# Token stage, laps and combination in one block, the last pair of experts added by products: a transformer program on one core

## The chip, the core and the metric

The program runs on one core of a Trainium2 chip. The core has five engines with their own instruction streams, which meet only in semaphores: TensorE (matrix products; PE in the profile, PEld its weight loads), VectorE (DVE), ScalarE (ACT), GpSimd (POOL) and SyncE (SP), which issues most DMA transfers. A transfer runs on 16 DMA engines and raises a semaphore by 16 when it has landed. The metric is the time of the whole program on the device in microseconds, lower is better.

## The reference

A transformer: first a block with experts that choose their tokens, then two layers (i = 0, 1), each of a mixer and a layer of experts chosen by the tokens, on 512 tokens of width 1024. All is in float32. What this case is about is the end of each of the two layers:

```python
# 4 groups of 8 experts: the best group of a token, and in it its 2 best experts
gates = group_probability * softmax(two best logits)
y     = sum over the 2 choices: gate * (silu(x @ w_gate[e]) * (x @ w_up[e])) @ w_down[e]
x     = layer_norm(ALPHA * x + y) * ln2_g + ln2_b      # ALPHA = 4 ** 0.25
```

There are 32 experts of inner width 512. Each gets as many tokens as chose it; none may be dropped.

## The kernel before

The tokens are four tiles of 128 (`NT`), the rows of the stream X are kept in SBUF. The layer's end is three stages, each a block of five engine programs that ends with a clearing of its semaphores and a barrier of all engines (`stage`, to line 219).

**`token_stage`** (from line 1841) goes over 16 pairs of experts. An expert has 64 slots (`SLOTS`), three pairs have an uneven split. For each pair TensorE gathers the tokens into slots by products with one-hot matrices (line 2089), multiplies by the gate and up weights (line 2119), VectorE forms silu(gate)*up (line 2013), TensorE turns it (2155) and multiplies by the down weights (2135), and ScalarE copies the result to `ye` (2057). GpSimd then writes the 128 rows of the pair to the table `expert_rows` in memory with an indirect transfer (1968), whose rows VectorE has counted (`rows_of_slots`, 1979 to 1981). The table was filled with zeros once, earlier in the program. The weights, 2 MB for each third of an expert's pair, go through a ring of 6 places and two further places (`more`), eight in turn; of the last pair the up and down weights come in halves, the second halves last (line 1952). At the stage's start VectorE finds the places of the experts and, in `rows_of_choices`, the table's row of every choice of every token (`at_row`) and the number of laps. After the weights SyncE issues the next mixer's first two loads (`load_until`, line 181), then the gate weights that a first lap would use (line 1959), and waits until the last rows are stored.

**`extra_slots`** (from 2498) holds the laps: where an expert was chosen by more tokens than it has slots, each lap computes 64 further rows. Its code is there for all counts; the engines load the count (line 2538) and branch over it when it is zero (2539). With the inputs of this case it is zero in both layers.

**`combine_and_norm`** (from 2659): ScalarE computes the exponentials of the gates, GpSimd gathers for each tile and each of the two choices 128 rows of 4 KB from `expert_rows` (line 2693) into three buffers, so that the fourth tile waits for the first to be added. For each tile ScalarE scales the first choice's rows (2716), VectorE adds the second's (2758) and ALPHA * X with the sum for the mean (2760), ScalarE takes the squares and the root (2722, 2724), and VectorE centres (2769) and scales (2775). In the first layer TensorE then turns the rows into columns (2709), after three idle products for each tile (line 190), and ScalarE copies them to `xT` (2730), on which the next mixer's first matmuls (4032) depend. In the second layer SyncE stores the tiles as the result (2684).

## Time and profile before

| | |
|---|---|
| median of 3 runs | 2883.49 us (2882.11 to 2886.49) |
| profiled execution, its own time | 2882.69 us |
| its span, first to last instruction | 2880.9 us |
| TensorE busy | 2576.0 us, 89% |
| VectorE busy | 904.4 us, 31% |
| ScalarE busy | 615.1 us, 21% |
| GpSimd busy | 271.9 us, 9% |
| mean granted TensorE clock | 0.953 of full |

How to read it: the span is one execution, its stages one after the other, so that a share of busy time is a mean over stages with different limits. The end of the first layer lies at 1945 to 1993 us, that of the second at 2834 to 2881. In the 40 slices of the page TensorE is at 8 tenths or less around the first and at 3 tenths in the very last slice.

### The profile page before, as it was taken

The page shows a single profiled execution, that of the slowest core. Times are in us where ns is not written, and L with a number is a line of the kernel's source. Part 1 is how long each engine was busy: PE and PEld are TensorE (multiplying, and loading weights), DVE is VectorE, ACT ScalarE, POOL GpSimd, SP SyncE. Part 2 cuts the span into 40 slices and gives each one's busy share as a digit, 9 for nine tenths or more (in the row PEclk, how much of TensorE's full clock was granted, in tenths as well). Part 3 has the DMA queues.
Part 4 walks back from the last instruction along what each step waited for, and adds up shares of the span by engine and source line. Part 5 has one row for each costly group of instructions (what it writes and reads, how often), then busy time and mean ns, then how long its engine had stood idle before and what let it go on. Part 6 is the DMA issues. An engine that isn't in the chain of part 4 may idle for free. (4 is left out here: it accounts for less than half of the span.)

```text
span 2880.9 us, 42912 instructions
## 1 busy us (share of the span) xinstructions
PE 2576.0 (89%) x17839; PEld 1316.3 (46%) x17839; DVE 904.4 (31%) x1996; ACT 615.1 (21%) x1192; POOL 271.9 (9%) x251
## 2 busy tenths in 40 slices
PE   7998788989999989998899989895998889999893
PEld 3544687444334434445454434442356554444341
DVE  2655574231122112456450101003335461010003
ACT  4412444221000101233110101102323221111012
POOL 0100453200000000001110000001004110000001
PEclk9999798889999999999999999998999999999996
DMA  8222200859999993000559999995004129999995
GB/s 317 94 96 108 76 3 17 346 228 427 427 428 429 429 400 128 23 1 30 194 214 427 426 427 428 427 401 195 8 1 182 49 88 404 427 427 428 427 426 221
DMA packets 111216, 737.17 MB, mean 256 GB/s; under 512 B 24388, under 2 KB 27824, under 8 KB 71744
## 3 DMA queue, kind: packets, MB, share of 16 engines
q1 hardware_dynamic: 102688, 704.21, 59.6%
q0 software_dynamic: 7776, 29.37, 2.6%
q8 instruction: 135, 2.21, 0.3%
q10 hardware_dynamic: 576, 1.05, 0.1%
q14 instruction: 41, 0.34, 0.0%
HBM read 709.40 MB, written 33.57 MB: 258 GB/s over the span
## 5 line engine op out<-in xcount | busy, mean ns | idle before, releaser
L2119 PE MATMUL bank<-ring,expert_in 128*64 128x512 f32 (+1 forms) x1792 | 343.2, 600 | 21.9 <-DMA ring<-in_moe_w_up_dram 21.2
L2013 DVE TENSOR_TENSOR hidden<-silu_gate,bank 128x512 f32<-128x512 f32 x32 | 33.7, 1053 | 630.2 <-PE bank L2119 396.8
L2119 PEld LDWEIGHTS bank<-ring,expert_in 128*64 128x64 f32 (+1 forms) x1792 | 113.3, 131 | 245.8 <-issue 245.5
L2135 PE MATMUL bank<-ring,hidden_T 128*64 128x512 f32 (+1 forms) x896 | 170.0, 595 | 31.0 <-ACT hidden_T L2053 31.0
L2089 PE MATMUL bank<-onehot,x_part 128*128 128x128 bf16 x3072 | 178.0, 220 | 0.0
L1747 PE MATMUL bank<-ring,expert_in 128*64 128x512 f32 x768 | 169.8, 598 | 4.9 <-DMA ring<-in_w_gate_dram 4.9
L2089 PEld LDWEIGHTS bank<-onehot,x_part 128*128 128x128 bf16 x3072 | 173.2, 98 | 1.6 <-issue 1.0
L2037 ACT ACTIVATE expert_in<-bank 128x512 f32<-128x512 f32 x64 | 35.0, 595 | 416.9 <-PE bank L2089 416.9
L2881 PE MATMUL bank<-ring,home 128*128 128x512 f32 x256 | 119.2, 628 | 3.5 <-PEq L219 3.5
L1968 POOL DMA_INDIRECT expert_rows<-expert_out,row_of_slot x32 | 31.3, 977 | 920.1 <-ACT expert_out L2057 920.1
L2119 PE MATMUL bank<-home,expert_in 128*64 128x512 f32 (+1 forms) x256 | 114.4, 600 | 0.0
L3225 PE MATMUL bank<-x_cols,ring 128*128 128x512 f32 x256 | 112.5, 593 | 1.3 <-PEq L219 1.3
L2135 PEld LDWEIGHTS bank<-ring,hidden_T 128*64 128x64 f32 (+1 forms) x896 | 52.1, 129 | 133.4 <-issue 96.7
L637 PE MATMUL bank<-home,ring 128*128 128x512 f32 (+1 forms) x320 | 111.7, 508 | 0.6 <-PEq L219 0.6
L1747 PEld LDWEIGHTS bank<-ring,expert_in 128*64 128x64 f32 x768 | 55.5, 138 | 116.5 <-issue 105.2
L4032 PE MATMUL bank<-x_cols,ring 128*128 128x512 f32 (+2 forms) x224 | 99.2, 608 | 1.4 <-PEq L219 1.4
L1762 PE MATMUL bank<-ring,hidden_T 128*64 128x512 f32 x384 | 85.9, 604 | 1.2 <-ACT hidden_T L1652 1.2
L2057 ACT ACTIVATE expert_out<-bank 128x512 f32<-128x512 f32 x64 | 34.7, 595 | 233.2 <-PE bank L2135 233.2
L682 PE MATMUL bank<-ring,home 128*128 128x512 f32 x192 | 84.4, 596 | 0.0
L190 PE MATMUL bank<-const 128*128 128x512 f32 x98 | 57.8, 733 | 28.7 <-DVE home L2760 24.7
L637 PEld LDWEIGHTS bank<-home,ring 128*128 128x128 f32 x320 | 60.5, 190 | 49.7 <-issue 45.9
L2881 PEld LDWEIGHTS bank<-ring,home 128*128 128x128 f32 x256 | 51.3, 203 | 68.4 <-issue 68.4
(684 smaller groups left out, 3907.4 us busy)
## 6 DMA issues: line engine op xcount, KB each, us to landing
ring<-in_moe_w_gate_dram SPq DMA_DIRECT2D x50, 2048.0 KB, 22.0
ring<-in_moe_w_down_dram SPq DMA_DIRECT2D x48, 2048.0 KB, 27.4
ring<-in_moe_w_up_dram SPq DMA_DIRECT2D x44, 2048.0 KB, 26.0
ring<-in_w_gate_dram SPq DMA_DIRECT2D x24, 2048.0 KB, 22.0
ring<-in_w_up_dram SPq DMA_DIRECT2D x24, 2048.0 KB, 21.1
ring<-in_w_down_dram SPq DMA_DIRECT2D x24, 2048.0 KB, 26.6
ring<-in_w_mod_dram SPq DMA_DIRECT2D x12, 2048.0 KB, 10.2
home<-in_moe_w_gate_dram SPq DMA_DIRECT2D x8, 2048.0 KB, 24.1
```

The costliest lines, as they stand in the source:

```text
L190: pe.matmul(self.psum[bank][:, :], self.c("ident"), self.const[:, 0:4, :], start=True, stop=True)
L637: mm = pe.matmul(B[g % 4][:, 0:SEGS[r][1]], m.slot(n)[:, k, f % 4 * P:f % 4 * P + P], aT[:, k, where[r]], start=(k == 0), stop=(k == NC - 1))
L682: mm = pe.matmul(B[g % 4][:, :], aT[:, k, t * P:(t + 1) * P], m.slot(m.in1[4 + s])[:, k, :], start=(k == 0), stop=(k == NC - 1))
L1747: mm = pe.matmul(B[2 + 2 * part + b][rows, :], xe[:, dc, rows], ws[e][:, c, b * COLS:(b + 1) * COLS], start=(dc == 0), stop=(dc == NC - 1))
L1762: mm = pe.matmul(B[6 + b][rows, :], hT[:, fc, rows], ws[e][:, c, b * COLS:(b + 1) * COLS], start=(fc == 0), stop=(fc == NF - 1))
L2037: return act.activation(xe[:, 4 * c:4 * c + 4, :], B[c][:, :].rearrange("p (c s) -> p c s", c=4), ACT.Copy)
L2089: mm = pe.matmul(B[c // 4][:, c % 4 * P:(c % 4 + 1) * P], src[part][:, t, c * P:(c + 1) * P], oh[:, t, :, :], start=(k == 0), stop=(k == 3 ...
L2119: mm = pe.matmul(B[2 + 2 * part][rows, :], xe[:, c, rows], ws[e][:, c, :], start=(c == 0), stop=(c == NC - 1))
L2135: mm = pe.matmul(B[6 + b][rows, :], hT[:, c, rows], ws[e][:, c, b * COLS:(b + 1) * COLS], start=(c == 0), stop=(c == NF - 1))
L2881: mm = pe.matmul(B[2 * (t % 2) + a][:, :], lhs(k)[:, t * P:(t + 1) * P], m.slot(n)[:, k, :], start=(k == 0), stop=(k == NC - 1))
L3225: mm = pe.matmul(B[g % 2][:, :], m.slot(n)[:, k, h * P:(h + 1) * P], xT[:, k, :], start=(k == 0), stop=(k == NC - 1))
L4032: mm = pe.matmul(B[job % 2][rows[0]:rows[1], :], m.slot(n)[:, k, at:at + size], xT[:, k, :], start=(k == 0), stop=(k == NC - 1))
```

## The change

The three stages become one, with one barrier at its end. In it:

- The gates and `rel`, the place of each choice relative to the last pair's slots, are computed at the start of the stage.
- The last pair isn't written to memory. VectorE builds for each tile a matrix of 128 tokens by 128 slots that holds the gate where a choice is in that slot (`last_onehots`), TensorE turns it (into `last_T`), and `scatter_last` multiplies it with `ye`. Its rows in the table stay zero.
- X is multiplied by ALPHA in the last pair. `choices` adds gate times the gathered row to it, directly for each choice; `add` then adds the products of the last pair from two banks, with the sums for the mean.
- The gathers go to the two places of the ring that the last pair doesn't use. The two of the first tile wait for the rows of the second to last pair to be stored; those of the other three also wait for the last pair's last weights to land.
- The laps' branch stands between the last pair and the combination in the program of every engine but GpSimd; a lap now adds its rows by products too. The first lap's weights are no longer loaded ahead.
- SyncE loads gain and shift of the norm after the last weights, and the next mixer's first two loads only when all gathered rows are added (`presummed`).
- One idle product fewer for each tile ahead of the transposes. Centring, scaling and square roots are as before; a square root without use loads its table ahead.

The diff, cut to its core (the code of a lap, the two removed functions, names and semaphores are left out):

```diff
-def token_stage(m, w, E, first_load, R, out_rows, first_lap, more, i):
+def token_stage(m, I, w, E, first_load, R, out_rows, more, i, X, xT=None, out=None):
...
+        at_row, g01, rel = R.at_row, R.g01, Q[0]
+        dead = K[1][:, :, :].rearrange("p a b -> p (a b)")
+        last_oh = dead[:, 0:NT * P].rearrange("p (t s) -> p t s", t=NT)
+        lane_last, last_tmp = dead[:, NT * P:(NT + 1) * P], dead[:, (NT + 1) * P:(NT + 2) * P]
+        last_T = act_g
...
+        place_of = lambda j: m.ring[:, (first_load + j) % RING, :]
+        y = [place_of(j).rearrange("p (t d) -> p t d", t=NT) for j in range(2)]
+        sq = more[1][:, 4:6, :].rearrange("p a b -> p (a b)")
+        spare = [a[:, :, :].rearrange("p c t -> p (c t)") for a in more]
+        held = [[place_of(j) for j in (2, 3, 4)], [place_of(5)] + spare]
...
+        def laps_beyond(eng, lap):
+
+            eng.wait_ge(laps_known, 2)
+            total = eng.value_load(R.count[0:1, 0:1], min_val=0, max_val=MOST_LAPS)
+            with eng.If(total > 0):
+                lap(total, 0, 0)
+                with eng.Fori(0, MOST_LAPS // 2 - 1) as k:
+                    with eng.If(total > 2 * k + 1):
+                        lap(total, 2 * k + 1, 1)
+                    with eng.If(total > 2 * k + 2):
+                        lap(total, 2 * k + 2, 0)
+                eng.nop()
...
+                laps_beyond(sp, lap)
+                sp.dma_start(gain, I["ln2_g_2"][i].partition_broadcast(P)).then_inc(ln_here, 16)
+                sp.dma_start(shift, I["ln2_b_2"][i].partition_broadcast(P)).then_inc(ln_here, 16)
+                sp.wait_ge(presummed, NT)
                 m.load_until(sp, end + 2)
-                sp.wait_ge(laps_known, 2)
-                e = sp.value_load(R.count[0:1, 1:2], min_val=0, max_val=E - 1)
-                sp.wait_ge(m.weights_used, base + loads * pairs - loads + 1)
-                src_w, chunks, cols = expert_loads(wg, wu, wd, e)[0]
-                sp.dma_start(first_lap[:, 0:chunks * cols].rearrange("p (c f) -> p c f", c=chunks), src_w).then_inc(m.lap_gate, 16)
-                sp.wait_ge(stored, 16 * pairs + stored_here)
+                sp.wait_ge(stored, 16 * (pairs - 1) + stored_here)
+                sp.wait_ge(ln_here, 32)
+                if out is not None:
+                    for t in range(NT):
+                        sp.wait_ge(shifted, t + 1)
+                        sp.dma_start(out[t * P:(t + 1) * P, :], X[:, t, :]).then_inc(out_stored, 16)
+                    sp.wait_ge(out_stored, 16 * NT)
...
-                for x in range(pairs):
+                for x in range(pairs - 1):
...
+                pool.wait_ge(gates_ready, 2)
+                pool.wait_ge(stored, 16 * (pairs - 1) + stored_here)
+                for t in range(NT):
+                    if t == 1:
+                        for e in range(2):
+                            _, last_here, before = home(loads * pairs - 2 + e, 1, 1)
+                            pool.wait_ge(last_here, 16 * (before + (loads * pairs - 1) // WIDE + 1))
+                    for j in range(2):
+                        pool.indirect_dma_start(y[j][:, t, :], None, out_rows[:, :],
+                                                bass.IndirectOffsetOnAxis(ap=at_row[:, t, j:j + 1], axis=0)).then_inc(here[2 * t + j], 16)
...
+                def last_onehots():
+
+                    dve.wait_ge(gathered, pairs)
+                    lo = Order(dve, last_order)
+                    dve.tensor_copy(lane_last[:, 0:SLOTS], R.lane[:, 0:SLOTS])
+                    lo.then(dve.tensor_scalar(lane_last[:, SLOTS:], R.lane[:, 0:SLOTS], float(SLOTS), None, ALU.add))
+                    for t in range(NT):
+                        dve.tensor_scalar(last_oh[:, t, :], lane_last, rel[:, t, 0:1], g01[:, t, 0:1], ALU.is_equal, ALU.mult)
+                        lo.then(dve.tensor_scalar(last_tmp, lane_last, rel[:, t, 1:2], g01[:, t, 1:2], ALU.is_equal, ALU.mult))
+                        last = dve.tensor_tensor(last_oh[:, t, :], last_oh[:, t, :], last_tmp, ALU.add)
+                        if t < NT - 1:
+                            lo.then(last)
+                        else:
+                            last.then_inc(last_ready, 1)
+                    for t in range(NT):
+                        dve.tensor_scalar(X[:, t, :], X[:, t, :], ALPHA, None, ALU.mult).then_inc(stretched, 1)
+
                 def pair(x):
-                    rows_of_slots(x)
-                    if not isinstance(x, int) or x < pairs - 1:
+                    if isinstance(x, int) and x == pairs - 1:
+                        last_onehots()
...
+                order.then(dve.tensor_tensor(rel[:, :, :], Q[0][:, :, :], Q[1][:, :, :], ALU.add))
+                order.then(dve.tensor_scalar(rel[:, :, :], rel[:, :, :], 1.0 - (E - 2) * SLOTS, None, ALU.add))
+                go = Order(dve, gate_order)
+                dve.wait_ge(exped, 2)
+                go.then(dve.tensor_reduce(mass[:, :, 0], R.below[:, :, :], AX_X, ALU.add))
+                go.then(dve.scalar_tensor_tensor(den[:, :, :], R.second[:, :, :], 1.0, mass[:, :, :], ALU.add, ALU.mult))
+                dve.reciprocal(g01[:, :, 0:1], den[:, :, :]).then_inc(gates_ready, 1)
+                dve.wait_ge(gates_ready, 1)
+                dve.tensor_tensor(g01[:, :, 1:2], g01[:, :, 0:1], R.second[:, :, :], ALU.mult).then_inc(gates_ready, 1)
+                dve.wait_ge(gates_ready, 2)
...
+                laps_beyond(dve, lap)
+                no = Order(dve, norm_order)
+
+                def choices(t):
+                    for j, told in enumerate((accumulated, presummed)):
+                        dve.wait_ge(here[2 * t + j], landed)
+                        if j == 0:
+                            dve.wait_ge(stretched, t + 1)
+                        else:
+                            dve.wait_ge(accumulated, t + 1)
+                        dve.scalar_tensor_tensor(X[:, t, :], y[j][:, t, :], g01[:, t, j:j + 1], X[:, t, :], ALU.mult, ALU.add).then_inc(told, 1)
+
+                def add(t):
+                    dve.wait_ge(presummed, t + 1)
+                    dve.wait_ge(scattered, t + 1)
+                    for h in range(2):
+                        cut = slice(h * COLS, (h + 1) * COLS)
+                        dve.scalar_tensor_tensor(X[:, t, cut], X[:, t, cut], 1.0, B[2 * (t % 2) + h][:, :], ALU.mult, ALU.add,
+                                                 accum_out=total[:, t, h:h + 1]).then_inc(summed, 1)
+                    dve.wait_ge(summed, 2 * t + 2)
+                    no.then(dve.tensor_tensor(minus[:, t:t + 1], total[:, t, 0:1], total[:, t, 1:2], ALU.add))
+                    dve.tensor_scalar(minus[:, t:t + 1], minus[:, t:t + 1], -1.0 / D, None, ALU.mult).then_inc(mean_ready, 1)
...
+                choices(0)
+                choices(1)
+                add(0)
+                choices(2)
+                add(1)
+                centre(0)
+                finish(0)
+                choices(3)
+                add(2)
+                centre(1)
+                finish(1)
+                add(3)
+                centre(2)
+                finish(2)
+                centre(3)
+                finish(3)
...
+                        act.wait_ge(last_turned, 1)
+                        act.activation(last_T[:, :], B[1][:, :], ACT.Copy).then_inc(last_T_ready, 1)
...
+                act.activation(R.below[:, :, :], R.below[:, :, :], ACT.Exp).then_inc(exped, 1)
+                act.activation(R.second[:, :, :], R.second[:, :, :], ACT.Exp).then_inc(exped, 1)
...
+                laps_beyond(act, lap)
...
+                act.activation(mass[:, 0, :], m.eps[:, 0:1], ACT.Sqrt)
+                root(0)
...
+                        pe.wait_ge(last_ready, 1)
+                        for t in range(NT):
+                            mm = pe.transpose(B[1][:, t * P:(t + 1) * P], last_oh[:, t, :], m.c("ident"))
+                        mm.then_inc(last_turned, 1)
...
+                laps_beyond(pe, lap)
+
+                def scatter_last(t):
+                    if t >= 2:
+                        pe.wait_ge(summed, 2 * (t - 1))
+                    for h in range(2):
+                        mm = pe.matmul(B[2 * (t % 2) + h][:, :], last_T[:, t * P:(t + 1) * P], ye[:, h * COLS:(h + 1) * COLS], start=True, stop=True)
+                    mm.then_inc(scattered, 1)
+
+                def turn_rows(t):
+                    if t >= 2:
+                        pe.wait_ge(x_copied, 2 * (t - 1))
+                    m.idle_products(pe, 4 + 2 * (t % 2), 2)
+                    pe.wait_ge(shifted, t + 1)
+                    for h in range(2):
+                        for c in range(4):
+                            at = (4 * h + c) * P
+                            mm = pe.transpose(B[4 + 2 * (t % 2) + h][:, c * P:(c + 1) * P], X[:, t, at:at + P], m.c("ident"))
+                        mm.then_inc(x_turned, 1)
+
+                pe.wait_ge(last_T_ready, 1)
+                pe.wait_ge(out_ready, pairs)
+                for t in range(NT):
+                    scatter_last(t)
+                    if xT is not None and t >= 2:
+                        turn_rows(t - 2)
+                if xT is not None:
+                    turn_rows(2)
+                    turn_rows(3)
...
-        whole = (m.moe2[i] + (E // 2) * len(pair_loads(*w, 0)) // WIDE * RING + 2) % RING
-        free = [m.ring[:, (whole + k) % RING, :] for k in range(4)]
-        held = [free[0:3], [free[3], own[:, :, :].rearrange("p c t -> p (c t)"), cols[:, :, :].rearrange("p c t -> p (c t)")]]
-        token_stage(m, w, E, m.moe2[i], R, S["rows"], held[0][0], more, i)
-        extra_slots(m, w, E, R.parts, R.lane, R.at_row, R.count, S["rows"], held, 16 * (i + 1))
-        combine_and_norm(m, I, i, S["rows"], R, X, cols, **ends)
+        token_stage(m, I, w, E, m.moe2[i], R, S["rows"], more, i, X, **ends)
```

## Rows read from the trace of the kernel before

**Rows 1.** the chain that ended last: start us, us, engine and line

```profile
2846.69 8.22 DMA chosen_rows<-expert_rows,row_of_choice
...
2856.27 1.29 DVE chosen_rows L2758
...
2857.59 1.24 DVE home L2760 x2
...
2874.76 1.28 DVE home L2769
...
2876.15 1.28 DVE home L2775
```

**Rows 2.** instructions by time, second layer's end: start us, us, engine, line

```profile
2834.35 0.59 PE L2135 MATMUL bank<-home,hidden_T 128*64 128x512 f32 x1
2835.01 1.08 ACT L2057 ACTIVATE expert_out<-bank 128x512 f32<-128x512 f32 x2 [7.21 <-PE bank L2135]
...
2877.46 0.33 SPq L2684 DMA_DIRECT2D out_dram<-home  x1
```

**Rows 3.** the same, first layer's end and the next mixer

```profile
1945.42 1.09 ACT L2057 ACTIVATE expert_out<-bank 128x512 f32<-128x512 f32 x2 [7.21 <-PE bank L2135]
...
1987.32 1.28 DVE L2775 SCALAR_TENSOR_TENSOR home<-home,ln_var 128x1024 f32<-128x1024 f32 x1
...
1990.73 1.08 ACT L2730 ACTIVATE x_cols<-bank 128x512 f32<-128x512 f32 x2 [2.88 <-PE bank L2709]
...
1992.54 19.98 PE L4032 MATMUL bank<-x_cols,ring 128*128 128x512 f32 x46 [1.42 <-PEq L219]
```

**Rows 4.** lines 2538 and 2539: ns min/median/max, first and last start us

```profile
L2538 PEldq TENSOR_LOAD <-laps x2: 315/401/487, 1952.5 to 2841.1; - x2
...
L2539 DVEq COMPARE_BRANCH  x2: 62/62/63, 1953.1 to 2841.7; - x2
...
L2539 PEldq COMPARE_BRANCH  x2: 3349/3430/3512, 1953.3 to 2841.8; - x2
```

**Rows 5.** instructions by time, start of the first layer's token stage

```profile
1491.09 0.90 DVE L2003 TENSOR_TENSOR onehot<-slot_lane,pair_slots 128x128 bf16<-128x128 f32 x4
...
1494.67 0.25 PE L2081 MATMUL bank<-one_bf,onehot 128*128 128x1 bf16 x4
```

**Rows 6.** lines 2990 and 392: VectorE from a bank, and scaling

```profile
L2990 DVE SCALAR_TENSOR_TENSOR home<-home,bank x16: 686/688/690, 1395.6 to 2344.2; 128x512 f32<-128x512 f32 x16
...
L392 DVE TENSOR_SCALAR x_rows<-x_rows,opening_rs x6: 749/750/753, 13.4 to 16.9; 128x1024 f32<-128x1024 f32 x6
```

**Rows 7.** DMA issues at 2813, 1958 and 2861 us: last number us to landing

```profile
expert_rows<-expert_out,row_of_slot POOLq DMA_INDIRECT x1, 7.9
...
chosen_rows<-expert_rows,row_of_choice POOLq DMA_INDIRECT x1, 7.8
...
chosen_rows<-expert_rows,row_of_choice POOLq DMA_INDIRECT x2, 5.3
```

**Rows 8.** issue of the last weights and their us to landing, both layers

```profile
2798.79 1.73 SPq L1952 DMA_DIRECT2D home<-in_moe_w_down_dram  x1
...
home<-in_moe_w_down_dram SPq DMA_DIRECT2D x1, 1024.0 KB, 29.5
...
1910.38 4.10 SPq L1952 DMA_DIRECT2D home<-in_moe_w_down_dram  x1
...
home<-in_moe_w_down_dram SPq DMA_DIRECT2D x1, 1024.0 KB, 30.0
```

**Rows 9.** stretches: busy of each engine, granted clock, DMA share, GB/s

```profile
2820.00:2825.00 5.00, 5.00 (x26) 1.45 (x22) 0.00 (x0) 0.00 (x0) 0.00 (x0) 1.00 1.02 424
...
2837.00:2840.00 3.00, 0.00 (x0) 0.00 (x0) 0.00 (x0) 0.00 (x0) 0.93 (x1) 0.52 0.15 56
...
1970.00:1973.00 3.00, 2.96 (x4) 1.42 (x5) 2.91 (x6) 2.76 (x5) 2.44 (x2) 0.50 0.37 127
```

**Rows 10.** DMA issue of the next mixer's first weights at 1921.9 us

```profile
ring<-in_od_w_in_dram SPq DMA_DIRECT2D x1, 1664.0 KB, 22.8
```

438 lines of the change are left out of this document (177 added, 261 removed).

## The prediction

> **What bounds the kernel now.** I began with the chain that ended last [rows 1]: the kernel ends in the combination of the second layer of token-choice experts, a series of VectorE instructions fed by a gather that lands 8.2 us after its issue at 2846.69. Next I read the instructions in order of time around that gather [rows 2]. The last product of the last expert pair starts at 2834.35, ScalarE copies it out at 2835.01, and the first addition of the combination begins only at 2856.27. So 21 us lie between the end of the products and the first useful addition, with TensorE idle. They hold the copy (1.1 us), the scatter of the last pair's rows to memory, two stage boundaries and the skipped lap code, and the 8.2 us of the gather. From 2856.27 VectorE is the bound until 2877.43, and the result's last store ends the span 3.47 us later. The first of the two layers has the same tail [rows 3]: copy at 1945.42, last VectorE instruction ends at 1988.60, next matmul of the following mixer at 1992.54. Nothing else in the program touches these two stretches, so the change is worth what it takes out of them, twice, plus or minus what it puts into the last pair and the start of the stage.
>
> One row explains most of the boundary: TensorE's branch over the lap code takes 3.43 us, behind a register load and checks of 0.6 us, where VectorE's takes 0.06 [rows 4]. No lap runs with this data (no matmul of a lap is in the trace), so all laps are only jumped over.
>
> **The change part by part.** All times are on the profiled run's scale; T0 is the moment when the first `add` of the new combination starts.
>
> Removed: the last scatter, two boundaries and their barriers, the load of the first lap's weights (2 MB a layer, read by nobody here), four ScalarE scalings.
>
> Start of the stage. VectorE gets two small instructions for `rel` and four for the gates, at about 0.2 us with their waits, 1.25 us. Before, it finished the second pair's one-hots at 1491.99 and TensorE asked for them at 1494.67 [rows 5]: 2.7 us of cover, 1.4 left. ScalarE's two exponentials and their table fall before the first half gathered. Cost 0; without that cover 1.25 us a layer.
>
> Last pair. `last_onehots` is 14 small instructions (about 3 us) and four scalings of X at 0.75 us [rows 6], 6 us, in a stretch where VectorE waited 22 us for the up products. TensorE's four transposes (0.66 us for four like them) sit in front of the hidden's transposes, for which it waited 1.3 us anyway; ScalarE's copy `last_T` falls beside the down products. Cost 0.
>
> The gathers of the first tile wait for the second to last pair's scatter, 7.9 us after its issue at 2813.6 [rows 7], so about 2821.5. They put 1 MB on engines that were full with weights: the last weights landed at 2798.79+29.5 = 2828.3 and at 1910.38+30.0 = 1940.4 [rows 8]. At the 424 GB/s of that stretch [rows 9] their 1.05 MB are 2.5 us. The delay of the last weights is thus between 0 and 2.5; I take 2.5, since the scatter beside full queues shows that the two share (7.9 us against 5.3 for a gather almost alone [rows 7]). The second halves of the down weights are wanted only in the middle of the products, near 2831.3, so TensorE doesn't stall at 2830.8. The page "DMA: Bandwidth & Descriptors" of the Trainium skill (SWDGE vs HWDGE vs iDMA) says that each DMA engine takes turns between the two kinds of queue; by that the gather gets its share at once and the weights pay the 2.5 us, while an order by issue would cost them nothing.
>
> The other six gathers queue on GpSimd behind the wait for these weights. Nothing else is on GpSimd, and VectorE waits for them. The second of tile 1 is issued 1.27 us after 2830.8, lands after 8.2 us [rows 1] (the layer-norm loads, 1 MB, now arrive at the same moment as before), and its addition takes 1.28: **2841.5**. In the first layer the same sum from 1940.4 is 1942.9+1.27+7.8 [rows 7]+1.28 = **1953.2**. Bounds: no delay and 5.3 us give 2836.2 and 1948.3.
>
> TensorE's path to the first addition: after the last product (2834.35) the 0.6 us and the branch of 3.43 [rows 4], then the two products of `scatter_last(0)`. A float32 product of 512 columns is two records, 0.43 us each at the upper clock (46 in 19.98 us [rows 3]), 0.87 at the lower. The granted clock had fallen to 1.2 GHz (0.52 of full) between 2837 and 2840 [rows 9], so I take the lower: 3.5 us. 2834.35+4.0+3.5 = **2841.9**; in the first layer 1944.76+4.0+3.5 = 1952.3. Bounds: no stall in the branch and the upper clock give 2836.1+1.9 = 2838.0; a fetch twice as long, since its transfer now meets gathers, gives 2845.3. The page "Runtime: NRT & Kernel Launch" (Instruction fetch mechanics) says that a taken branch to a target outside the loaded instructions waits for a fetch; by it the skip, now longer, stalls TensorE again, and perhaps VectorE and ScalarE too.
>
> So T0 is 2842.0 and 1953.2: two paths that arrive within 1 us of each other.
>
> Chain from T0, VectorE without a gap: four `add` at two 0.69 us instructions from a bank [rows 6] with accumulation and 0.35 for the mean, 1.75 each; two `choices` still to come (tiles 2 and 3), 2x1.32 us by the spacing of 2856.27 and 2857.59 [rows 1]; four centre and finish, 2.65 each (2874.76 to 2877.43 [rows 1]). 7.0+5.3+10.6 = 22.9. Before it was 21.2: the additions of two tiles have gone ahead of T0, but those of the other two and the bank additions stay in it.
>
> Second layer: 2842.0+22.9+3.47 = 2868.4 against 2880.9, **-12.5**. First layer: 1953.2+22.9 = 1976.1; the tail after VectorE was 3.94 us (1988.60 to 1992.54 [rows 3]), of which 1.2 go with one idle product fewer ahead of the last transposes: 1978.8 against 1992.54, **-13.7**. The next mixer's first weights (`load_until(end + 2)`) are now issued after the last `choices`, T0+11.4 = 1964.6, on idle engines; 14 us are left for 1.8 MB, so nothing.
>
> Sum: -26.2. The profiled run's own time was 2882.7, 0.8 below the median of the runs: 2856.5+0.8 = **2857**.
>
> **The rivals.**
> (a) Both paths to T0 arrive at their lower bounds: 2838.0 and 1948.3, so -16.5 and -18.6: **2848**. For it: the lap load is gone and the transfers total the same, and a branch costs 0.05 us on the others. Against: the 3.43 us were seen twice.
> (b) The branch's fetch takes twice as long beside gathers, and TensorE enters the next mixer at the lower clock for some 2.5 us: -9.2, -11.2, +2.5, **2866**.
> (c) The next mixer's weights decide. They took 22.8 us to land before [rows 10], behind full queues. From 1964.6 that is 1987.4: the first layer keeps only -5.1, **2866**. Against it: nothing else is on the queues then.
> (d) The change doesn't do what it says: the gathers don't run ahead of the end of the products but start when the rows are out, 2836. Then T0 is 2849.5 (8.2, 1.27 and two `choices` later) and about 1959.5: **2871**.
> (e) Slower than before: TensorE goes through the new tail in short pieces and the granted clock doesn't come back when the next mixer starts. Its matmuls then take twice their time; from 26 us of full-speed work done at half speed the gain is gone, and with 30 it is **2887**. Against: after 24 idle us, at the lower clock from 1970 to 1973 [rows 9], the clock was back before the next mixer.
>
> **How the numbers follow.** The forecast has 0.72; (a) 0.11, (b) 0.06, (c) 0.04, (d) 0.02, (e) 0.03, and 0.02 that it stays within 0.2%. A measurement of this kernel can tell 0.2% (5.8 us) from no change. The own range of the likeliest, one or two steps of the two paths early or late, is 2850 to 2863; with most of (a) and (b) it is 2848 to 2865. Faster 0.95, same 0.02, slower 0.03.
>
> **What would show it.** Right: one stage where three were; the first gather issued near 2821 and 1932, the third near 2831 and 1943; a TensorE branch of 3.4 us right behind the last down product; VectorE without gaps from the first bank addition on. The steps to check first are the landing of the last weights, the branch, the clock in `scatter_last(0)`, and whether the mixer's first matmul waits for its weights. The prediction is wrong if the last pair's own products wait for weights, or if VectorE stands still inside the 22.9 us.

## The result and the profile after

The changed kernel took 2847.4 us (median of four runs, 2844.2 to 2849.2), the kernel before 2883.7 on the same chip: ratio 0.9872, 95% interval 0.9855 to 0.9889. That is a gain of 36 us where 26 were predicted, and just outside the range (2848). On two more chips the same pair gave 0.9888 (0.9871 to 0.9906) and 0.9886 (0.9865 to 0.9906). The mean of the three ratios, 0.9882, is 34 us; so the first comparison showed a little too much, and the prediction (0.9908) was still 7 to 8 us short.

The page of the changed kernel, sections 1 and 3 (busy time; DMA queues with packets, MB and share):

```profile
span 2842.4 us, 42947 instructions
...
PE 2583.4 (91%) x17871; PEld 1320.7 (46%) x17871; DVE 929.7 (33%) x2064; ACT 607.8 (21%) x1188; POOL 269.8 (9%) x249
...
q1 hardware_dynamic: 102400, 700.01, 60.0%
q0 software_dynamic: 7488, 29.10, 2.6%
```

The profiled run took 2844.2 us itself, 3.2 under its median, against 2882.7 before: 38.5 us between the two profiles. The end of the chain that ended last, in the profile after (start, us, engine and line):

```profile
2774.13 32.77 DMA home<-in_moe_w_down_dram
2807.03 3.67 PE bank L2394 x16
2812.63 3.29 PE bank L2486 x4
2816.03 1.32 DVE home L2207 x4
2817.65 1.29 DVE home L2200
...
2836.91 1.28 DVE home L2224
```

and the same stretch by instructions, with the idle time ahead of them and who ended it:

```profile
2800.45 0.66 PE L2414 MATMUL bank<-const,rank_pairs 128*128 128x128 f32 x4
...
2807.03 0.61 PE L2394 MATMUL bank<-spare_weights,hidden_T 128*64 128x512 f32 x1 [0.29 <-DMA home<-in_moe_w_down_dram]
...
2810.73 1.08 ACT L2270 ACTIVATE expert_out<-bank 128x512 f32<-128x512 f32 x2 [7.21 <-PE bank L2394]
...
2812.63 7.08 PE L2486 MATMUL bank<-expert_out,silu_gate 128*128 128x512 f32 x12 [1.95 <-ACT expert_out L2270]
...
2813.20 2.67 DVE L2200 SCALAR_TENSOR_TENSOR home<-ring,gate,home 128x1024 f32<-128x1024 f32 x2 [2.89 <-DMA ring<-expert_rows,row_of_choice]
...
2816.03 0.69 DVE L2207 SCALAR_TENSOR_TENSOR home<-home,bank 128x512 f32<-128x512 f32 x1
...
2838.22 0.33 SPq L2037 DMA_DIRECT2D out_dram<-home  x1
```

To be seen: the last weights release TensorE's second half of the down products (2807.03, the line of [rows 8]). ScalarE's copy starts at 2810.73, TensorE's products that scatter the last pair at 2812.63, and the first bank addition (T0) at 2816.03, 5.3 us after the copy's start, where the kernel before needed 21 us to its first addition [rows 1, 2].

For everything that follows a layer's end is cut at four marks: the first of the last down products, ScalarE's copy of the last pair, T0, and VectorE's last instruction; behind it comes the next mixer's first product (first layer) or the end of the span (second layer). The expectations below call the part from the copy on a tail. Of the 38.5 us between the two profiles, 16.3 lie from the copy to the next mixer in the first layer (47.1 to 30.9) and 14.2 from the copy to the end in the second (45.9 to 31.7), 30.5 together. The other 8 lie where the prediction had put nothing: 2.7 ahead of the first of these copies and 5.4 in the mixer, router and token work between the two ends (842.5 to 837.1). Of those 5.4, 3.3 are one stretch of the mixer. Windows of before and after over the same work (busy of each engine, granted clock, DMA share, GB/s):

```profile
2032.00:2056.00 24.00, 24.00 (x56) 11.30 (x56) 17.64 (x21) 3.73 (x5) 0.00 (x0) 0.86 0.00 1
```

```profile
2013.00:2034.00 21.00, 21.00 (x57) 10.32 (x56) 16.41 (x19) 3.87 (x6) 0.00 (x0) 1.00 0.00 1
```

TensorE is busy all the time in both; the clock was 0.86 of full in one and full in the other. So three things are open: whether these 8 us belong to the change, why T0 comes 5.3 us behind the copy and not 7.0, and what the branch, the gathers' landing and the order of the transfers have to do with it.

### The profile page after: what moved, and what is told of

It is laid out like the page before. It is cut to its first block and busy times, and to the rows that moved or that the text cites. A ratio compares the mean times of both kernels' runs of the same rounds, so it can differ in the third digit from the quotient of the medians.

```text
span 2842.4 us, 42947 instructions
## 1 busy us (share of the span) xinstructions
PE 2583.4 (91%) x17871; PEld 1320.7 (46%) x17871; DVE 929.7 (33%) x2064; ACT 607.8 (21%) x1188; POOL 269.8 (9%) x249
## 5 line engine op out<-in xcount | busy, mean ns | idle before, releaser
L2394 PEld LDWEIGHTS bank<-ring,hidden_T 128*64 128x64 f32 (+1 forms) x896 | 52.1, 129 | 133.4 <-issue 96.7
L636 PEld LDWEIGHTS bank<-home,ring 128*128 128x128 f32 x320 | 60.5, 190 | 49.7 <-issue 45.9
L1572 DVE TENSOR_TENSOR home<-home,bank 128x512 f32<-128x512 f32 x64 | 43.8, 687 | 119.9 <-PE bank L1773 119.9
## 6 DMA issues: line engine op xcount, KB each, us to landing
ring<-in_moe_w_gate_dram SPq DMA_DIRECT2D x48, 2048.0 KB, 22.9
```

Source lines behind the costliest of these rows:

```text
L636: mm = pe.matmul(B[g % 4][:, 0:SEGS[r][1]], m.slot(n)[:, k, f % 4 * P:f % 4 * P + P], aT[:, k, where[r]], start=(k == 0), stop=(k == NC - 1))
L1572: dve.tensor_tensor(X[:, t, cut], X[:, t, cut], B[4 + dh][:, :], ALU.add).then_inc(added, 1)
L2394: mm = pe.matmul(B[6 + b][rows, :], hT[:, c, rows], ws[e][:, c, b * COLS:(b + 1) * COLS], start=(c == 0), stop=(c == NF - 1))
```

## The experiments

Each kernel is compared with the kernel before on its own chip. The times of a single kernel spread over 5 to 19 us here (the changed kernel on the third chip: 2843.2 to 2858.3), more than most effects asked for, so the verdicts rest on the marks of the profiles, one profile for each altered kernel. This table has them all, in us; the first column of each layer is the whole end, from the first last-down product on. The changed kernel's own three profiles differ by up to 1.3 us in one of these columns and by 1.5 in the last. The four kernels from "all gathers wait" to "last pair through the table" ran on a chip that has no profile of the changed kernel.

| kernel | ratio (95%) | layer 1: end | copy to T0 | layer 2: end | copy to T0 | both ends |
|---|---|---|---|---|---|---|
| before | | 54.3 | | 53.0 | | 107.3 |
| before, second profile | | 56.8 | | 55.5 | | 112.3 |
| changed | 0.9872 (0.9855-0.9889) | 38.7 | 6.0 | 39.3 | 5.3 | 78.0 |
| changed, second | 0.9888 (0.9871-0.9906) | 37.8 | 5.1 | 39.6 | 4.9 | 77.4 |
| changed, third | 0.9886 (0.9865-0.9906) | 37.4 | 4.7 | 39.1 | 5.0 | 76.6 |
| branch bare | 0.9923 (0.9907-0.9939) | 43.2 | 10.5 | 46.2 | 11.9 | 89.4 |
| layer-norm loads late | 0.9900 (0.9883-0.9917) | 40.4 | 7.8 | 39.4 | 6.0 | 79.8 |
| all gathers wait | 0.9903 (0.9879-0.9927) | 39.3 | 7.3 | 40.7 | 7.2 | 80.0 |
| no gather waits | 0.9894 (0.9872-0.9917) | 38.8 | 5.8 | 41.3 | 7.1 | 80.1 |
| lap load back | 0.9902 (0.9879-0.9925) | 40.6 | 7.9 | 43.5 | 9.8 | 84.1 |
| last pair through the table | 0.9916 (0.9894-0.9937) | 42.8 | | 44.5 | | 87.3 |
| free gathers, new order | 0.9879 (0.9856-0.9902) | 36.7 | 5.8 | 40.1 | 7.2 | 76.9 |
| the same, warm | 0.9871 (0.9850-0.9892) | 36.1 | 5.7 | 37.6 | 5.9 | 73.7 |
| the same, no branch | 0.9879 (0.9857-0.9900) | 37.8 | 3.7 | 39.0 | 3.7 | 76.9 |

(The second profile of before is of one run that took 2892.9 us, just above what that kernel took in eleven runs beside it, 2878.1 to 2891.9. Its ends are longer by 1.7 us a layer because the first of its last down products ran at a lower clock: 8.9 us from the first of them to the copy, not 7.2.)

**Is the rest of the gain the change's?** Both kernels once more, unaltered.

> The changed kernel once more, unaltered. Open: the 5.4 us that the profiles show in the mixer, router and token work between the two tails (842.5 before, 837.1 after) and 2.7 us ahead of the first tail. If they belong to the change (a clock that comes back sooner in the next mixer), this profile shows the same: from the first layer's copy of the last pair plus its tail to the second layer's last copy again 837 us. If they are chance of one execution, that stretch is anywhere between 836 and 843 and the dip of the clock seen before at 2032 to 2056 appears or not without rule. Time 2847 in either case, ratio 0.987.

> The kernel before once more, unaltered, for a second profile. If the dip of the granted clock (0.86 between 2032 and 2056, worth 3.3 us) belongs to the longer idle tail, it is there again and the stretch between the tails is again 842 us; if it is chance, this profile has it elsewhere or not, and the stretch is between 836 and 843.

The stretch between the two ends took 842.5 and 843.2 us in the two profiles of before, and 837.1, 842.1 and 842.1 in the three of the changed kernel; in the other kernels of the table, all with the new ends, anything from 836.3 to 841.7. The copy of the first layer started at 1945.4 and 1953.3 before, at 1942.8, 1948.5 and 1938.1 after. So the same kernel differs from itself by 5 us between the ends and by 8 to 10 ahead of them. The 2.7 us ahead of the ends are within that. The 3.3 us in the mixer are chance: to one and the same ScalarE instruction behind the dip (`gate_abs`) it was 65.5 and 63.8 us from the mixer's first product before, and 62.1, 65.5 and 65.5 in the changed kernel. But the stretch as a whole isn't shown to be chance: all twelve profiles with the new ends are shorter there (mean 839.4) than both profiles of before (mean 842.9). Some 3.5 us may belong to the change; two profiles of before are few, and what would cause it is open. Between copy and next mixer or end it is 93.0 and 94.6 us before against 62.5, 61.2 and 60.9 after: 31 to 34.

**Where does the branch lie?**

```diff
+                pe.wait_ge(out_ready, pairs)
                 laps_beyond(pe, lap)
```

> TensorE waits for ScalarE's copy of the last pair before it enters the skipped lap code; nothing else is changed. Theory A (the sequencer runs ahead of its products, so the branch of 4.7 to 5.2 us lay beside the last products and beside the copy): the branch now begins at the copy's end, 1.1 us after the last product, and the first product of the last pair's scatter comes 3.4 to 5 us later, the whole chain of VectorE with it: +7 to +10 us over both layers, 2854 to 2857. Theory B (the branch begins behind the last product, as my prediction had it, and cost its 4 us already): it moves by the copy's 1.1 us at most and so does the start of the additions: +0 to +2, 2847 to 2849.

TensorE's branch over the lap code in the second layer, in the changed kernel and then with the wait; ns, and when it started:

```profile
L1964 PEldq COMPARE_BRANCH  x1: 4664/4664/4664, 2807.8 to 2807.8; - x1
```

```profile
L1964 PEldq COMPARE_BRANCH  x1: 5982/5982/5982, 2820.9 to 2820.9; - x1
```

and the instructions behind it, in the kernel with the wait:

```profile
2827.03 2.90 PE L2487 MATMUL bank<-expert_out,silu_gate 128*128 128x512 f32 x3 [8.09 <-issue]
...
2830.89 0.69 DVE L2207 SCALAR_TENSOR_TENSOR home<-home,bank 128x512 f32<-128x512 f32 x1 [7.08 <-PE bank L2487]
```

In the changed kernel the branch starts 2.9 us before the copy does, while the last down products still run; it ends at 2812.5, 0.7 us after the copy's end. Put behind the copy, it delays the scatter's products by its whole length: T0 comes 10.5 and 11.9 us after the copy instead of about 5, both ends 12 us longer, the ratio 0.0035 (10 us) worse. Theory A, above its bounds (7 to 10); the branch itself took 4.5 and 6.0 us. TensorE's sequencer runs ahead of its products: the register load ahead of the branch started at 2807.1, right when the wait for the last weights was passed and 3.6 us before the copy could start.

**What sets the landing of the second tile's gathers?**

```diff
                 laps_beyond(sp, lap)
+                for e in range(2):
+                    _, last_here, before = home(loads * pairs - 2 + e, 1, 1)
+                    sp.wait_ge(last_here, 16 * (before + (loads * pairs - 1) // WIDE + 1))
                 sp.dma_start(gain, ...)
```

> The loads of the layer norm's gain and shift (1 MB a layer) are issued only when the last weights have landed, at the same moment as the gathers of the second tile. Theory A (these gathers landed in 5.5 us and not in the 8.2 predicted because the layer-norm loads, issued 28 us earlier, were through by then): the gathers of the second tile take about 8 us to land, and the last weights land up to 2.5 us earlier; the start of the additions moves by +0 to +2.7 a layer, total 2847 to 2853. Theory B (the landing has nothing to do with these loads; the second scatter and lap load that are gone made the difference): 5.5 us again, start of the additions where it was or 0 to 2 us earlier, total 2843 to 2847.

The two gathers of the second tile, first layer, in the changed kernel's second profile and then with late layer-norm loads (last number: median us to landing):

```profile
ring<-expert_rows,row_of_choice POOLq DMA_INDIRECT x2, 5.1
```

```profile
ring<-expert_rows,row_of_choice POOLq DMA_INDIRECT x2, 8.0
```

8.0 us beside these loads, 5.1 without: theory A. In the second layer it is 7.1 to 7.7 against 4.8 and 5.5. T0 came 7.8 and 6.0 us after the copy, where the prediction had 7.8 and 7.0 for the changed kernel. Not all of that is the gathers': the branch took 6.9 and 6.4 us in this kernel, and both paths to T0 were late by the same amount. Both ends together are 2.5 us longer than in the changed kernel (77.3, mean of three), all of it in the first layer; in the second the last weights landed 31.0 us after their issue, without a stall, and that paid for the later T0.

**Was the removed lap load worth nothing?**

```diff
+                sp.wait_ge(laps_known, 2)
+                e = sp.value_load(R.count[0:1, 1:2], min_val=0, max_val=E - 1)
+                sp.wait_ge(m.weights_used, base + loads * pairs - loads + 1)
+                sp.dma_start(lap_weights(0, 0), expert_loads(wg, wu, wd, e)[0][0]).then_inc(lap_extra, 16)
                 laps_beyond(sp, lap)
                 sp.dma_start(gain, ...)
```

> The load of the first lap's weights (2 MB a layer, read by nobody here), which the change had removed and which my prediction priced at nothing, is put back in its old place, ahead of the layer-norm loads. Theory A (its bytes push what is behind it): the layer-norm loads land 4 to 5 us later, together with the gathers of the second tile, which then take about 8 us to land as they did beside the late layer-norm loads; the start of the additions moves by 2 to 3 us a layer: total +4 to +6 against the changed kernel. Theory B (priced rightly at nothing): landing of these gathers 4.5 to 6.5 us as before, total unchanged within 2 us.

SyncE's DMA issues in the second layer of this kernel (start, us to issue):

```profile
2786.08 3.41 SPq L2012 DMA_DIRECT2D home<-in_moe_w_down_dram  x1
2805.79 0.33 SPq L2031 DMA_DIRECT2D ring<-in_moe_w_gate_dram  x1
2806.95 0.34 SPq L2033 DMA_DIRECT2D ln_gain_and_shift<-in_ln_g_dram  x1
```

and of the changed kernel:

```profile
2774.13 4.02 SPq L2011 DMA_DIRECT2D home<-in_moe_w_down_dram  x1
2778.97 3.15 SPq L2028 DMA_DIRECT2D ln_gain_and_shift<-in_ln_g_dram  x1
```

and what the gather of the second tile then takes in the chain of the kernel with the load:

```profile
2821.04 10.47 DMA ring<-expert_rows,row_of_choice
2832.73 1.31 DVE home L2213 x4
```

10.5 us to landing, T0 7.9 and 9.8 us after the copy, both ends 6.8 us longer than the mean of the three profiles of the changed kernel (77.3). Theory A, above what it expected (4 to 6). The rows show a part that neither theory had: the lap load waits on SyncE for the first products of the last pair to free its place, 16 us after the weights ahead of it, and the layer-norm loads stand behind it. Taking it away took 2 MB from the engines, and it also let 1 MB of other loads start 16 us earlier (4.8 us after the last weights' issue instead of 20.9). How the 6.8 us divide is not shown. Layer-norm loads that were later still (the run above) cost 2.5 alone, and the 2 MB themselves were under way beside the gathers: in the first layer the lap load was issued at 1931.4 and landed 19.0 us later, at 1950.4, when the second tile's gathers (1945.3 and 1946.6) were out.

```profile
ring<-in_moe_w_gate_dram SPq DMA_DIRECT2D x1, 2048.0 KB, 19.0
```

So the larger part is probably the bytes, the smaller the queue. The timed runs, 0.9902 against 0.9872 to 0.9888, are right in sign and don't resolve it.

**Do the gathers have to wait for the weights?**

```diff
-                    if t == 1:
+                    if t == 0:
                         for e in range(2):
                             _, last_here, before = home(loads * pairs - 2 + e, 1, 1)
                             pool.wait_ge(last_here, ...)
```

> The gathers of the first tile wait for the last weights too; nothing else changes. Measured by the tails: from ScalarE's copy of the last pair to the next mixer's first product (30.0 and 30.9 us in two profiles of the changed kernel) and from the copy to the end (31.7 and 31.2). Theory A (the first tile's megabyte pushes the last weights back by 2 to 3 us): the weights now land after about 29.5 us instead of 32 to 33, TensorE's stall in the last down products is gone, and since the gathers start that much earlier after the products the start of the additions moves by less than 1.5 us: tails within 1.5 us of before, total within 3 us of the changed kernel. Theory B (the weights are late for another reason): they land after 32 to 33 us again, and the second tile's gathers, now third and fourth in the line, come 2.5 us later: tails +2.5 each, total +5.

The last weights landed 31.3 us after their issue in the second layer (32.8 to 33.2 in the changed kernel), the stall in the down products (0.3 to 1.0 us) was gone, T0 moved from 5 to 7.2 us after the copy, and both ends are 2.7 us longer together. From the copy on, as the theories were put, it is 2.0 and 2.1 us a layer: between A (under 1.5) and B (2.5), with the weights between them too; they gained 1.5 to 1.9 us of the 3 that A gave them. Nor need the late landing be all the gathers' doing: in the second profile of before the last weights of that layer took 31.4 us with no gather beside them.

With the wait left out altogether:

```diff
-                    if t == 1:
-                        for e in range(2):
-                            _, last_here, before = home(loads * pairs - 2 + e, 1, 1)
-                            pool.wait_ge(last_here, ...)
```

> No gather waits for the last weights: all eight are issued as soon as the second to last pair's rows are stored. Theory A (weights and gathers share the engines by bytes): 3 MB more meet the last weights, which land 3 to 7 us later, and TensorE stalls that long in the middle of the last down products. VectorE's order keeps two of its additions behind the start, so nothing is won there but the 1 us that the second tile's gathers had cost: total +4 to +12 against the changed kernel. Theory B (the weights' queue goes ahead of the gathers): weights as before, 32 to 33 us, no stall beyond 0.5 us, start of the additions 4 us after the copy instead of 5 to 6: total -2 to -4.

TensorE went on with the last weights 32 and 33 us after their issue, as in the changed kernel, and not 3 to 7 us later: theory A failed. The DMA queues between 2807.7 and 2814.5, in which six gathers were issued while the last weights were under way (packets, MB, share of the engines' time):

```profile
q1 hardware_dynamic: 294, 1.41, 50.6%
q0 software_dynamic: 361, 1.34, 49.9%
...
ring<-expert_rows,row_of_choice POOLq DMA_INDIRECT x6, 12.5
```

The two kinds of queue had half of the engines' time each. The page "DMA: Bandwidth & Descriptors" of the Trainium skill (SWDGE vs HWDGE vs iDMA) says that an engine takes turns between them; this trace agrees. Why six more gathers hardly delay the weights is seen in the same 7 us of both kernels, from 8 to 1 us before the weights land: in the changed kernel with the first tile's two gathers,

```profile
q1 hardware_dynamic: 325, 1.69, 58.6%
q0 software_dynamic: 241, 0.90, 34.1%
```

and with all gathers free:

```profile
q1 hardware_dynamic: 315, 1.60, 55.5%
q0 software_dynamic: 317, 1.19, 43.9%
```

Two gathers took a third of the engines' time and left some of it unused. Eight took that too, and little of the weights' share: 1.60 MB against 1.69. They land 12 us after their issue instead. But theory B's gain (-2 to -4) didn't come either: the ends are 2.8 us longer. What is late is the branch:

```profile
L1964 PEldq COMPARE_BRANCH  x1: 5998/5998/5998, 2815.8 to 2815.8; - x1
```

6.0 us here and 5.2 in the first layer, against 3.4 to 5.2 (six branches, mean 4.1) in the changed kernel; it ends 1.4 and 2.0 us after the copy. During each branch the profile has one or two packets, 16 KB each, on the queue that it calls instruction; that they wait among the gathers is inferred from the branch's length, not seen. The page "Runtime: NRT & Kernel Launch" of the Trainium skill (Instruction fetch mechanics) says that a taken branch out of the loaded window waits for its fetch. TensorE's branches agree, with 3.4 us where the DMA engines were nearly idle and up to 6.9 beside full queues. The load isn't the only cause: in the second profile of before one took 4.8 us with the engines busy 5% of the time.

```profile
L2539 PEldq COMPARE_BRANCH  x2: 3564/4166/4767, 1960.3 to 2851.3; - x2
```

**How much is the block, how much the products?**

```diff
-                for x in range(pairs - 1):
+                for x in range(pairs):
                     pool.wait_ge(rows_known, x + 1)
...
-                pool.wait_ge(stored, 16 * (pairs - 1) + stored_here)
+                pool.wait_ge(stored, 16 * pairs + stored_here)
...
-                    scatter_last(t)
...
-                        dve.scalar_tensor_tensor(X[:, t, cut], X[:, t, cut], 1.0, B[2 * (t % 2) + h][:, :], ALU.mult, ALU.add,
-                                                 accum_out=total[:, t, h:h + 1]).then_inc(summed, 1)
```

The one-hots of the last pair, their transposes and their copy go too, and VectorE takes a tile's choices, mean, centre and finish in turn.

> One block as in the change, but the last pair again goes through the table: its rows are scattered, and all eight gathers wait for that; no products scatter it, and VectorE has no additions from a bank. It tells how much of the gain is the block and how much the products. By the rows of the changed kernel: copy's end to the scatter's landing 1 + 5.3 us, two gathers issued and landed 7, so the first addition comes 14.5 us after the copy's start + 1.1; then VectorE has 8 additions (10.6), four means and four centre and finish (11.4): copy to the last VectorE instruction 37.6 against 27.3 to 28.1, so each tail +9 to +10, total +19, ratio 0.995 to 0.996. If the block alone had brought most of the gain, the tails would be longer by under 5 us each; if it had brought nothing, by 15.

Both ends 87.3 us, 10 longer than in the changed kernel and 20 shorter than before: the block brought two thirds of what the ends gave (20.0 of 30.0 us against the first profile of before), and the products, with the early gathers that they allow, one third. I had expected 19 and a ratio of 0.995 to 0.996, and it is 0.9916. GpSimd in the second layer of this kernel:

```profile
2826.31 0.98 POOL L2046 DMA_INDIRECT expert_rows<-expert_out,row_of_slot  x1 [22.31 <-ACT expert_out L2252]
2829.72 0.97 POOL L2056 DMA_INDIRECT ring<-expert_rows,row_of_choice  x1 [2.42 <-DMA expert_rows<-expert_out,row_of_slot]
```

and VectorE's first addition there:

```profile
2834.05 1.28 DVE L2189 SCALAR_TENSOR_TENSOR home<-ring,gate,home 128x1024 f32<-128x1024 f32 x1 [18.21 <-DMA ring<-expert_rows,row_of_choice]
```

A scatter with nothing beside it landed in 2.6 us, not the 5.3 that I had taken from a gather, and the first gather in 4.3; the first addition comes 9.7 us after the copy, not 15.6.

**A faster version?** Three kernels on one chip with the changed kernel. The first lets all gathers go and adds the third tile's choices ahead of the first bank addition:

```diff
-                    if t == 1:
-                        for e in range(2):
...
                 choices(1)
+                choices(2)
                 add(0)
-                choices(2)
```

> No gather waits for the last weights, and VectorE adds the third tile's choices ahead of the first bank addition instead of behind it; nothing else changes against the changed kernel. The run with free gathers alone had its sixth gather on GpSimd issued at 1943.1 and 2811.5 and landing 11 to 12 us later, and the first bank addition at 1956.4 and 2825.8, held by TensorE's branch and products. Theory A (the third tile's rows are there by then and the chain behind gets two additions, 2.7 us, shorter, 22.2 to 19.5): tails of 28.0 and 30.8 us (copy to the next mixer's first product, copy to the end) against 30.0 to 30.9 and 31.2 to 31.7 in the changed kernel: total -3 to -4. Theory B (gathers issued earlier only land later, so the third tile's choices now hold the first bank addition up): tails as in the changed kernel or 1 us longer, total within 2 us.

28.9 and 32.1 us from copy to next mixer and to the end: the first layer 0.7 to 2 us shorter, the second 0.5 to 0.9 longer. Between the theories. The chain from T0 was 20.4 and 20.7 us where 19.5 was worked out. The windows behind the last down products of the second layer (busy of each engine, granted clock, DMA share, GB/s) show why:

```profile
2814.00:2816.00 2.00, 0.66 (x4) 0.00 (x0) 1.05 (x2) 1.27 (x3) 0.00 (x0) 1.00 0.94 373
2816.00:2818.00 2.00, 0.00 (x0) 0.00 (x0) 1.90 (x2) 1.30 (x2) 0.00 (x0) 0.75 0.72 287
2818.00:2820.00 2.00, 1.97 (x3) 0.96 (x4) 1.90 (x3) 0.00 (x0) 0.00 (x0) 0.50 0.33 135
```

TensorE stood still behind the last down products, and its clock was at the lower of its levels (0.50) when the scatter's products began; VectorE waited for them inside the chain. The second kernel gives TensorE work there:

```diff
+                m.idle_products(pe, 4, 2)
                 laps_beyond(pe, lap)
```

> As the run before in this series (free gathers, third tile first), and TensorE makes two idle products right behind the last down products, ahead of the skipped lap code, so that it works while ScalarE copies and its sequencer waits for the branch. Theory A (the granted clock falls to its lower level in the 2 us of idleness behind the last down products, and that doubles the first products of the last pair's scatter): from the first product of the scatter to the first bank addition it is 1.9 us instead of 3.2 to 3.9, the tails are 1.3 to 1.9 us shorter each, total -3 against the free-order kernel. Theory B (the clock falls all the same, or the rows of the third tile arrive last): no change in the start of the additions, total within 1 us.

```profile
2811.00:2813.00 2.00, 2.00 (x7) 0.68 (x4) 1.23 (x2) 1.16 (x3) 0.00 (x0) 1.00 0.96 385
2813.00:2815.00 2.00, 0.70 (x2) 0.00 (x0) 1.88 (x2) 1.42 (x2) 0.00 (x0) 1.00 0.73 291
2815.00:2817.00 2.00, 1.80 (x5) 0.88 (x6) 1.90 (x3) 0.00 (x0) 0.00 (x0) 1.00 0.31 127
```

The clock stayed at full, the chain was 19.5 us in both layers, and the ends are 3.2 us shorter together than in the kernel without the idle products, 2.9 to 4.3 shorter than in the changed kernel. TensorE's gap ahead of the scatter, without and then with the idle products (second layer):

```profile
2818.03 4.61 PE L2482 MATMUL bank<-expert_out,silu_gate 128*128 128x512 f32 x5 [3.37 <-issue]
```

```profile
2815.20 3.24 PE L2483 MATMUL bank<-expert_out,silu_gate 128*128 128x512 f32 x7 [1.50 <-issue]
```
From the scatter's first product to T0 it was 3.0 and 2.5 us, not 1.9: now the third tile's rows hold T0. By the timed runs the ratio is 0.9871 (0.9850 to 0.9892) beside 0.9886 (0.9865 to 0.9906) for the changed kernel on that chip; the intervals overlap, so the 3 us are seen in the marks of one profile and not in the time.

The third leaves TensorE's lap code out of that kernel; with this data no lap runs, so nothing of the computation is missing.

> As the warm kernel, and TensorE's lap code is left out, its branch with it (a kernel for this data only: no lap runs, the result doesn't need it). It tells what the branch still costs. In the run with free gathers it took 5.2 and 6.0 us and ended 1.4 and 2.1 us after ScalarE's copy. Theory A (what sticks out of the cover is all that it costs): the first product of the scatter comes within 0.2 us of the copy's end, the tails are 0 to 2 us shorter than in the warm kernel, less where the third tile's rows arrive last: total -1 to -4. Theory B (the branch costs its whole 4 to 5 us): tails shorter by 4 each, total -8.

T0 comes 3.7 us after the copy in both layers instead of 5.7 and 5.9, which looks like theory A, with 2 us for what stuck out. But the end as a whole was 77, not 70 us: in this profile TensorE stalled 2.8 us for the last weights in both layers (34.4 and 35.7 us to landing) and then ran its products at a clock of 0.74:

```profile
2825.00:2830.00 5.00, 5.00 (x17) 1.59 (x18) 2.36 (x3) 0.04 (x1) 0.00 (x0) 0.74 0.72 291
```

The median, 2850.1, shows no gain over the warm kernel's 2847.2. Nor do the 2 us belong to the branch for certain. In the warm kernel the third tile's rows held T0, and taking the branch out doesn't by itself make them earlier; here the late weights moved the copy to 11.3 and 11.6 us behind the issue of these rows' last gather, where it had been 7.3 and 7.6, so that they were there in time. What the branch still costs is thus open. Why the weights came later I can't say; it was one profile, of the slowest of this kernel's six runs. It does show the gathers ahead there: in the last 7.8 us before the weights landed they had 76.1% of the engines' time in the second layer and the weights' queue 25.3%, against 47.9% and 52.1% in the warm kernel.

The profile of the changed kernel on this chip, whose copy to T0 and ends are in the table:

> The changed kernel unaltered, on the same chip as the three above, for their comparison: tails of 30 to 31 and 31 to 32 us, the stretch between the tails anywhere from 836 to 843, ratio between 0.987 and 0.990.

## Why the prediction fell short, step by step

**What held.** One block for three; the sign; no slower by the clock, none of the rivals (b) to (e). From T0 on VectorE has no gap: 22.2 us in all six ends of the changed kernel, 22.9 predicted (an addition from the bank with its mean took 1.62 us, not 1.75). From VectorE's last instruction to the next mixer's first product 2.7 us, as predicted; to the end of the span 4.2 instead of 3.5, 0.7 given back. The next mixer's weights landed 7 us after their issue and were there before TensorE. The start of the stage cost nothing: its one-hots were ready at 1489.7, TensorE took them at 1491.2. The last weights came later, as foreseen: from 29.5 and 30.0 us [rows 8] to 32.8 and 31.8, 3.3 and 1.8 where 2.5 was taken. How much of it is the first tile's gathers is less sure, since 29.4 to 31.4 us were seen without them. The first gather was issued 13.1 and 13.6 us ahead of the copy (14 and 13 predicted).

**What failed: the 8.2 and 7.8 us for the second tile's gathers.** The prediction took them from [rows 1, 7] with the words "the layer-norm loads, 1 MB, now arrive at the same moment as before". They didn't. Before, they stood on SyncE behind the lap load and two stage boundaries; now both are gone, and they were issued at 2779.0, 29 us before these gathers. The gathers landed after 4.5 to 6.5 us. Two runs bear it out: with late layer-norm loads it is 7 to 8 us, with the lap load back, its own 2 MB and the layer-norm loads behind them, 10.5 in the second layer. The lap load is the one edit that the prediction left out of its sum, and put back it cost 6.8 us in both ends together, by its bytes and by what stood behind it on its queue. The term is 1.4 to 2.7 us a layer smaller than it was taken; the second gather's issue, 2 us after the weights' landing and not 1.27, takes back 0.7.

**What failed: the branch "right behind the last down product".** It starts 2.6 to 2.9 us ahead of the copy, beside them, and is mostly covered by the products and the copy: with the branch put behind the copy both ends lengthen by 12 us. The prediction's TensorE path had 0.6 + 3.43 after the last product; in its place stands the copy, and the scatter's products began 1.2 us after the copy's start in four of the six ends, and 1.9 and 2.7 in the two where the branch took 4.7 and 5.2 us. The 3.5 us for its first two products at the lower clock were right (3.29 in the chain shown above). In five of six ends it is now the second tile's additions that end last before T0.

**Also failed, small.** "TensorE doesn't stall": it stalled in the middle of the last down products, 0.3 to 1.0 us by the idle time in the rows, and from their first to the copy it was 0.5 to 1.2 us longer than before. For the first layer the prediction's own numbers held a stall: the products there began at 1938.3 and want the second halves 3.5 us later, at 1941.7, while it had them landing at 1942.9.

**The sum.** Copy to T0 was to be 7.0 and 7.8 us; the means of three profiles are 5.1 and 5.3, so -1.9 and -2.5. The chain is 0.75 shorter twice, the end of the span 0.7 later. That is -5.2, and 26.2 + 5.2 = 31.4, against 31 to 34 in the profiles from the copy on. The stalls take back 1.3, so that 30 is left of the whole ends, as in the table (107.3 to 77.3). The mean of the three comparisons is 34. The 4 us between are about what the stretch between the two ends differs by in the mean (3.5); no run shows what causes it, so this part of the gain stays open. The first comparison's 36.3 lies above the others' by no more than single executions differ. The rival that came nearest is (a), both paths to T0 at their lower bounds: its T0 of the second layer was 3.0 us after the copy's start, the measured one 5.1. Its time, 2848, was met by half of its mechanism, the stretch that nobody priced and some luck of the first chip.

## What to carry to other kernels

A transfer or a wait that is taken out is priced by its own bytes and by what stands behind it on its queue, even if nobody reads it: list the next issues of that engine and ask what they will meet when they start earlier. A branch of TensorE belongs to its sequencer: its cost is what sticks out behind the last wait it had to pass plus its fetch, so look for the row of the branch's start, and keep waits away from in front of it. When single executions differ by 10 us, cut the trace at marks around the change and compare these pieces over several profiles before explaining a total.

## What the hardware showed that was not expected

The skip of the lap code on TensorE took 3.4 to 6.9 us, longer as a rule the more the DMA engines carried beside it: 3.4 to 3.6 with the engines 2 to 5% busy, and once 4.8; 3.4 to 5.2 in the changed kernel (62 to 72% busy), 5.1 to 6.1 with all gathers free (82 to 92%), 6.4 and 6.9 with the layer-norm loads beside it; VectorE, ScalarE and SyncE took 0.05 to 0.06 for theirs. An indirect transfer of 0.5 MB landed in 4.1 to 5.5 us next to little, in 8 to 11 beside full queues, in 12 to 13 behind others of its kind, and a scatter alone in 2.6. With two idle products (2.0 us of TensorE's time) behind the last product the granted clock was still at 1.00 after the 1.5 us of idleness that were left; without them TensorE was idle for 3.4 us, and the clock was at 0.50 when it began again.
